# Reordering the seven products of a Strassen group, and when its weight sums are made

## The reference

```
h   = x + concat(mlstm(...), hgrn2(...)) @ w_out        # gates, conv, norms around it
h   = h + sigmoid(rms(h) @ w_pg) * (p @ w_pe);  x = rms(h)
proj = rms(x) @ w_in_2                                   # u, v, q, k, v_att, g_a, g_b
merged = sigmoid(g_a) * (y_a @ w_up_a) + sigmoid(g_b) * (y_b @ w_up_b)
x   = x + merged @ w_o
x   = x + (silu(h @ w_gate) * (h @ w_up)) @ w_ffn_out    # FFN_HIDDEN = 5632
x   = x + sigmoid(rms(x) @ w_ple_gate) * (p @ w_ple)
```

## Time and profile before

| | |
|---|---|
| three runs | 1892.29, 1894.62, 1895.87 us (median 1894.62) |
| the profiled execution | 1893.05 us, span of its instructions 1891.3 us |
| busy | TensorE 99%, VectorE 78%, ScalarE 60%, GpSimd 7% |
| granted TensorE clock | 0.999 of full on average |
| DMA | 535.95 MB, mean 283 GB/s |

### The profile page before, as it was taken

One profiled execution on the slowest core, in us unless ns is written; L12 is line 12 of the kernel. 1 busy time (PEld: TensorE's weight loads), 2 busy tenths in 40 slices (PEclk: granted clock), 3 DMA queues, 4 the chain that ended last, 5 costly groups with the idle time before them and its releaser, 6 DMA issues.

```text
span 1891.3 us, 23371 instructions
## 1 busy us (share of the span) xinstructions
PE 1877.2 (99%) x9018; PEld 1641.9 (87%) x9018; DVE 1471.8 (78%) x1591; ACT 1140.8 (60%) x1417; POOL 130.4 (7%) x156
## 2 busy tenths in 40 slices
PE   9999999999999999999999999999999999999998
PEld 8888888888888888888888888888888888888887
DVE  6889776655666677778888657988998999898865
ACT  7556445555566556566766455666766676666553
POOL 4000011000001100000000000000000000000000
PEclk9999999999999999999999999999999999999999
DMA  9799898999989879998797886788878887987653
GB/s 392 267 284 310 274 309 272 330 347 327 309 290 312 271 269 299 321 315 278 295 313 247 330 256 239 254 311 284 276 254 320 280 271 257 327 260 249 219 188 130
DMA packets 86815, 535.95 MB, mean 283 GB/s; under 512 B 10416, under 2 KB 11184, under 8 KB 40752
## 3 DMA queue, kind: packets, MB, share of 16 engines
q1 hardware_dynamic: 72736, 458.69, 63.3%
q0 software_dynamic: 13824, 75.50, 20.6%
q10 hardware_dynamic: 144, 0.26, 0.0%
HBM read 529.69 MB, written 105.38 MB: 336 GB/s over the span
## 4 chain that ended last, share of the span: by engine, by line
PE 90%; DVE 5%; DMA 3%; issue 1%; ACT 1%; POOL 0%; SPq 0%; ACTq 0%; DVEq 0%; POOLq 0%
PE acc L1359 44%; PE acc L1364 22%; PE aux L1724 12%; PE aux L1728 6%; DVE wlo L2556 2%; PE aux L1338 2%; DMA ple<-in_w_ffn_in 1%; DVE wlo L1876 1%; PE aux L1431 1%; DVE ple L2551 1%; DMA ple<-in_w_in 1%; DMA raw<-summed 1%; PE aux L1805 0%; ACT whi L928 0%; ACT whi L1177 0%
## 5 line engine op out<-in xcount | busy, mean ns | idle before, releaser
L1876 DVE TENSOR_TENSOR wlo<-raw,whi 128x1024 fp32r<-128x1024 f32 x512 | 623.8, 1226 | 296.4 <-ACT whi L928 288.4
L928 ACT ACTIVATE whi<-raw 128x1024 fp32r<-128x1024 f32 x511 | 534.0, 1054 | 449.8 <-PE acc L1364 414.1
L1359 PE MATMUL acc<-whi,actA_hi 128*128 128x512 f32 x892 | 344.0, 386 | 0.7 <-ACT whi L928 0.7
L1359 PE MATMUL acc<-whi,actA_lo 128*128 128x512 f32 x892 | 339.1, 380 | 0.0
L1359 PE MATMUL acc<-whi,actB_hi 128*128 128x512 f32 x796 | 304.5, 383 | 0.2 <-DVE actB_lo L2673 0.2
L1359 PE MATMUL acc<-whi,actB_lo 128*128 128x512 f32 x796 | 301.7, 379 | 0.0
L1177 ACT ACTIVATE whi<-ple 128x1024 fp32r<-128x1024 f32 x192 | 201.0, 1055 | 139.4 <-PE acc L1364 55.6
L2556 DVE TENSOR_TENSOR wlo<-ple,whi 128x1024 fp32r<-128x1024 f32 x192 | 230.2, 1220 | 31.3 <-ACT whi L1177 28.5
L1364 PE MATMUL acc<-wlo,actA_hi 128*128 128x512 f32 x892 | 229.1, 379 | 0.0
L1364 PE MATMUL acc<-wlo,actB_hi 128*128 128x512 f32 x796 | 204.4, 379 | 0.0
L2556 DVE TENSOR_TENSOR wlo<-raw,whi 128x1024 fp32r<-128x1024 f32 x144 | 174.2, 1220 | 30.6 <-ACT whi L1177 28.9
(11 more groups left out here) (366 smaller groups left out, 2377.0 us busy)
## 6 DMA issues: line engine op xcount, KB each, us to landing
raw<-in_w_in SPq DMA_DIRECT2D x108, 1024.0 KB, 7.3
raw<-in_w_ffn_out SPq DMA_DIRECT2D x44, 1024.0 KB, 6.9
summed<-in_w_ffn_in POOLq DMA_DIRECT2D x36, 1024.0 KB, 11.6
raw<-in_w_ffn_in SPq DMA_DIRECT2D x72, 512.0 KB, 7.9
ple<-summed SPq DMA_DIRECT2D x24, 1024.0 KB, 4.9
raw<-summed SPq DMA_DIRECT2D x48, 512.0 KB, 5.4
ple<-in_w_ffn_in SPq DMA_DIRECT2D x18, 1024.0 KB, 6.9
ple<-in_w_ffn_in POOLq DMA_DIRECT2D x36, 512.0 KB, 9.9
```

What stands on the lines that cost most here:

```text
L928: act.activation(whi[:, g % RING], raw_piece(g), ACT.Copy).then_inc(hi_ready, 1)
L1359: pe.matmul(acc2(n)[:, t, :], act[x][:, k + c, t * P:(t + 1) * P], woven(whi, g, c), start=(p == 0 and c == 0 and x == 0), stop=False)
L1876: dve.tensor_tensor(wlo[:, g % RING], raw_piece(g), whi[:, g % RING].bitcast(F32), ALU.subtract)\
```

## The change

- `S_ORDER` becomes M1, M2, M5, then M6 and M3 in turns (q by q), M7, M4. All that hung on "the last of M3" as the end of the four (`s_gates`, the gate's activation, the return of `resid`) now hangs on M7's last quarter, which stands where M3's last one stood. The wait for the forms of the activations is at M5 now.
- The copy `s_fifth` is made one piece earlier.
- The four DRAM sums at the first merge pieces go from `SUM_AT`; numbers 40 to 43 take the places in the output product (g 419 to 437), numbers 44 to 47 are at g 443, 449, 455 and 461, the first FFN pieces. Before the FFN's norm factor GpSimd issues those with g below `g_ffn` only.
- Three small ones: the norm factor's product at `L0 + 31`; the second half of `ml_cols` after the next piece (`ml_rows_spread`); the product of the slab uB 2 two pieces later.

```
-S_ORDER = [(m, q) for m in ("M1", "M2", "M7", "M5") for q in range(4)] \
-    + [("M6", 0), ("M6", 1), ("M3", 0), ("M6", 2), ("M3", 1), ("M6", 3), ("M3", 2), ("M3", 3)] + [("M4", q) for q in range(4)]
+S_ORDER = [(m, q) for m in ("M1", "M2", "M5") for q in range(4)] \
+    + [(m, q) for q in range(4) for m in ("M6", "M3")] + [(m, q) for m in ("M7", "M4") for q in range(4)]
...
-        SUM_AT += [PLAN.g_plan + 1 + 4 * i for i in range(4)]
         SUM_AT += [PLAN.g_out + 11 + 6 * i for i in range(4 * S_GROUPS - len(SUM_AT))]
...
                 if name == "ffn":
-                    add_in_dram(len(SUM_AT))
+                    add_in_dram(len([g for g in SUM_AT if g < PLAN.g_ffn]))
...
-                if g == S_AT[c, "M5", 3] + 3:
+                if g == S_AT[c, "M5", 3] + 2:
                     s_done(act, c, "M5")
...
-                for i in range(2):
-                    u = AUX[("bc", i)]
-                    free(u)
-                    for h in range(2):
-                        ins = pe.matmul(bank(u)[:, h * S:(h + 1) * S], sel[:, 2 * i + h, :], hrow[:, 3, :], start=True, stop=True)
-                    ins.then_inc(aux_full, 1)
+            def ml_rows_spread(i):
+                u = AUX[("bc", i)]
+                free(u)
+                for h in range(2):
+                    ins = pe.matmul(bank(u)[:, h * S:(h + 1) * S], sel[:, 2 * i + h, :], hrow[:, 3, :], start=True, stop=True)
+                ins.then_inc(aux_full, 1)
...
                     if (s, p) == (10, 7):
                         ml_cols()
+                        ml_rows_spread(0)
+                    if (s, p) == (11, 0):
+                        ml_rows_spread(1)
...
-                        if w == L0 + 30:
+                        if w == L0 + 31:
                             powered(dve, f"hB{half}")
...
-                s_done(dve, c, "M3")
+                s_done(dve, c, "M7")
...
-                        if g == slab_end(role, j) + (2 if slab_end(role, j) in PLAN.block_end else 3):
+                        last = slab_end(role, j)
+                        if g == last + (2 if last in PLAN.block_end else 5 if (role, j) == ("uB", 2) else 3):
                             u_product(role, j)
```

More of the change, by code:

```diff
@@ L801, in _ @@
                     sp.wait_ge(lo_ready, free + 1)
-                    sp.wait_ge(piece_used, S_AT[M_GROUPS - 1, "M3", 3] + 1)
+                    sp.wait_ge(piece_used, S_AT[M_GROUPS - 1, "M7", 3] + 1)
                     sp.wait_ge(sem("resid_held"), 16)
@@ L1224, in _ @@
                     s_copies(g, c)
-                    if g == S_AT[c, "M3", 3] + 7:
+                    if g == S_AT[c, "M7", 3] + 7:
                         act.wait_ge(sem("s_gate_in"), c + 1)
@@ L1296, in _ @@
                 split_hi(g)
-                if g == S_AT[S_GROUPS - 1, "M3", 3] + 7:
+                if g == S_AT[S_GROUPS - 1, "M7", 3] + 7:
                     s_silu(S_GROUPS - 1)
@@ L1699, in s_piece @@
                     pe.wait_ge(sem("tr_taken"), fills_before(g, "a"))
-                if m == "M7" and q == 0:
+                if m == "M5" and q == 0:
                     pe.wait_ge(sem("merge_forms_lo" if c < M_GROUPS else "forms_lo"), 4)
@@ L2635, in _ @@
                         s_up(c)
-                    if g == S_AT[c, "M3", 3] + 3:
+                    if g == S_AT[c, "M7", 3] + 3:
                         s_gates(c)
```

## The result

The changed kernel takes 1940.16 us (median of 6, 1937.51 to 1942.12), the kernel before 1894.37 us in the same comparison (median of 6, 1892.29 to 1895.87): ratio 1.0242, 95% interval 1.0229 to 1.0255. The forecast was 1886 us with a range of 1882 to 1893. It was wrong in sign and by 54 us. The case that happened is rival D, to which the prediction gave 0.07, and it came out more than twice as large as D's own price (54 us above the forecast, where D had 20).

What follows compares the result with a forecast made beforehand. TensorE was taken as the bound, busy 1877.2 of 1891.3 us, with only its losses to win: -6.9 + 0.7 - 0.6 - 1.6 = -8.4 from 1893.05 gives 1884.65, plus 1.57 to the runs' median, 1886 us; range 1882 to 1893.

Steps and rivals of the forecast that it cites:

- rival D: M7's last quarter late beside accumulating DMAs in every group, from a landing of 7.6 us on: 20 us lost, 1906; chance 0.07.
- Scaling 4.4 by 9.3 / 6.8 gives 6.0 us, which is hidden.: "Seventh" landing alone, scaled by b21's landing beside accumulating DMAs over b22's: under the 7.6 us available to M7's last quarter.
- the prediction's term for M7: M7's quarters, at distances of about 14.3, 13.0, 9.1 and 7.8 us, lose nothing; group 0's old 1.62 us go.
- The Trainium skill's rule: DMA engines alternate between queues with work: "seventh" up to 8.8 us, 1.2 us lost per group, 14 us, 1900 us in all.
- rival B: VectorE late in the stretch of sums, 0.4 to 0.9 us in each FFN group: 1890 to 1894 us; chance 0.12.
- M4, -5.3 us: M4's accumulating DMAs get 16.9 us of distance instead of 10.4, so all six M4 losses go.
- M7 of group 0, -1.6 us: Longer distances and no DRAM sums competing at the first merge pieces: group 0's loss of 1.62 us at M7 goes.
- The DRAM sums, "Cost 0; at worst 1.1 us": Four sums moved to the FFN's beginning cost nothing; at worst group 3 again loses what it lost, 1.1 us.
- rival C: DMAs stay late elsewhere, at M5 or M6's sums; half of 6.9 us returns, some at FFN's start: 1890 to 1893; chance 0.09.
- "Fifth" and b22, cost 0: Loads due sooner: "fifth" for M5 has 14.3 us, slowest landing 12.8; cost 0. b22's median landing 6.8 against 10 us.
- VectorE, +0.7 us: Sums and splits from M5's third quarter to M3's third: small losses over all groups, bounds 0 and 12 x 1.2 us.
- The norm factor's product and the gates' rows, -0.6 and -1.6: Product made behind the operands near 161 us: TensorE's wait goes, -0.6; gates' rows split in halves: clock stays up, -1.6 us.

Runs made afterwards that it cites:

- experiment 5: The changed kernel with GpSimd's twelve times four accumulating DMAs made plain, same place and bytes, the addition left out: 1891.39 us, ratio 0.9988 to the kernel before.
- experiment 4: The changed kernel with each group's third and fourth accumulating DMA issued later, when M7's first and second quarter are split: 1908.16 us, ratio 1.0071.
- experiment 9: As experiment 8, but in the order M1, M2, M7, M5 and M6 woven, M3, M4: 1891.85 us, ratio 0.9987 to the kernel before.
- experiment 10: The order of experiment 9 and the three small edits, with the DRAM sums where they were before the change: 1889.68 us, ratio 0.9975.
- experiment 11: As experiment 10, with the merge's four DRAM sums placed where the DMA share is lowest: 1887.64 us, ratio 0.9968 to the kernel before.
- experiment 1: The changed kernel with the old group order back; moved DRAM sums and small edits stay: 1897.78 us, ratio 1.0013 to the kernel before.
- experiment 8: The kernel before with the three small edits, the last eight DRAM sums all in the output product, and their copies no longer ahead of `resid` and `p` loads: 1897.17 us.
- experiment 6: The changed kernel with each accumulating DMA cut from 512 KB to 256 KB, half the addition left out: 1893.14 us, ratio 1.0001 to the kernel before.
- experiment 2: The changed kernel with the four DRAM sums back at the first merge pieces, new order kept: 1934.56 us, ratio 1.0213 to the kernel before.
- experiment 3: The changed kernel without the twelve groups' accumulating DMAs, the second term of M4's weights left out: 1890.13 us, ratio 0.9977 to the kernel before.
- experiment 7: The kernel before with the three small edits alone, order and sums as before: 1891.25 us, ratio 0.9987; 1890.27 us in one more run.

## Why the prediction was wrong

*The step that failed* is the landing of "seventh" in rival D: "Scaling 4.4 by 9.3 / 6.8 gives 6.0 us, which is hidden." With it the prediction's term for M7 counted no loss but the old one of group 0. Measured are 11.3 us for the third quarter and 10.2 for the last (medians of twelve), 5.9 and 7.0 for the first two. Three things were wrong in it.

- The ratio came from the wrong pair. b22's 6.8 us was no undisturbed landing: these loads were issued right behind a 1 MB load, with the DMA share at 0.89. And the scaling was not needed. b21's loads move the same 512 KB in the place to which "seventh" was to go, beside the accumulating DMAs, as the kernel before shows in group 3:

```profile
1217.49 1.85 POOL L898 DMA_DIRECT2D ple<-in_w_ffn_in  x2 [66.36 <-DVE wlo L2556]
...
1219.94 9.06 SPq L788 DMA_DIRECT2D raw<-in_w_ffn_in  x4
```

The last two accumulating DMAs follow at 1221.4 and 1226.0. The landings of these b21 loads are the 9.3 us of the earlier trace rows, and as they stand they are over D's 7.6 us.
- A ratio of landings is no sum of work. By the engine times of experiment 5 the burst of group 5 holds 4 x 2.9 for the accumulations, 4 x 1.4 for "seventh" and 2.8 for the std load, 20 us of all 16 engines. It starts at 1356.0, and its last quarter lands at 1380.2. M7's third quarter needed its weights at 1375.7 less ScalarE's 1.06, 18.6 us after the start. With plain DMAs in the same places (experiment 5) the burst is 14 us, and TensorE does not wait. The comparison is rough: what was issued up to and with the third quarter's load is only 15.7 us. But by its landing at 1378.6 the engines had worked 21 us (the shares of the stretches above), so the transfers issued behind it took their part, and in the first 8 us the share was only 0.57 and 0.92. Nothing in a sum over one transfer shows that; the sum over the burst does, and the prices were there in the earlier trace rows, if only roughly.
- The quarter looked at was the last, since its distance is the shortest. The third has 1.3 us more of it, but the end of its wait comes first, and then the last finds its weights nearly there.

The Trainium skill's rule, which the prediction weighed and set aside ("DMA: Bandwidth & Descriptors", Queues, rings and completion order), was nearer to the truth than my scaling, and still not enough: by it 4.4 us becomes up to 8.8, while the third quarter's landings are 11.3 us in the median and 12.6 at most. Experiments 4 and 5 show what it leaves out here: how many transfers the burst holds, and that those of the other queue take twice their bytes' time.

*The size.* D's 20 us took 1.7 us for each group. The waits at M7 are 31.3 us, some 2.8 us for each of eleven groups; with that come 7.8 us of clock, which D did not count, and VectorE's share: its splits, held up with ScalarE's, arrive in a heap, and the waits of TensorE's weight loads for `wlo` at L1731 are 12.1 us in 20 places against 4.7 in 8. Without the accumulating DMAs they are 2.4 in 4, so that is a consequence and not rival B.

*M4, -5.3 us:* right in mechanism, but the size was that of one execution. In the changed kernel 0.4 us of wait for its loads is left, and the order of experiments 9 to 11, which gives M4 two more quarters and keeps M7 where it was, has it as a gain: 1889.68 against 1891.25 us with sums and small edits the same (two comparisons, whose intervals overlap), and by rows no wait for `ple<-in_w_ffn_in` where the small edits alone left 29.4 us. By starts M4 loses 3.7 us in the trace of the small edits alone and nothing in that of experiment 10.

*M7 of group 0, -1.6 us:* half right. It had been the sums (experiments 1, 8 and 11: no loss with the sums moved away, the first two in the old order). But the same M7 waits 2.94 us, in its third quarter, by the new order.

*The DRAM sums, "Cost 0; at worst 1.1 us":* wrong, 5.5 us. It went by the number of pieces between the sums and did not ask what else is issued there. At the FFN's beginning the first group loads its `r1` and four slots at once. It is the place that rival C names, with 1890 to 1893 us, 4 to 7 above the forecast.

*"Fifth" and b22, cost 0:* right apart from group 3, where M5 loses 1.85 and 0.87 us by starts, beside the sums. The 12.8 us of the earlier trace rows are passed there; the landings of all 24 "fifth" loads of the changed kernel are

```profile
DMA to landing us min/median/max: 4.6/4.9/17.3
```


*VectorE, +0.7 us:* can't be read off, since its waits in the changed kernel follow from the late loads. With plain DMAs, in the same order, the waits for `wlo` are 5.0 us in 9 places, 0.3 more than before. Right as far as that shows.

*The norm factor's product and the gates' rows, -0.6 and -1.6:* right, -2.5 us together with the third small edit, as far as an interval of -4.2 to -0.8 can say. What the prediction took there from the Trainium skill ("TensorE: Matmul & The Clock Gate", Part 1), that the place varies from run to run, the page says of the clock's rise. That its fall varies too is shown by the traces (below); the sum did not use it.

## What to carry to other kernels

Where a change brings loads nearer to each other, add up the DMA time of the whole burst, each transfer at its own price, and compare it with the time from the burst's first issue to its first need (here 20 against 18.6 us with waits, 14 without); neither a landing time nor the mean DMA share tells it. An accumulating DMA goes into that sum at twice its bytes. Where loads of the same size already stand beside the same traffic, take their landing as it is, without scaling, as the least. When TensorE waits some microseconds, the half clock behind the wait may come on top (8.7 us behind five waits here).

## What the runs showed of the hardware

- A DMA that adds to its destination took 2.9 us of all 16 DMA engines for 512 KB, a plain one from the same queue 1.4 us, and one that adds 256 KB 1.5 us (experiments 5 and 6). The median landings are 9.1 and 5.7 us (all 48).
- With the DMA share at 1.0, the rate in the burst was 271 to 307 GB/s with accumulating DMAs. With plain ones it was, in the same burst

```profile
1346.00:1350.00 4.00, 4.00 (x20) 3.52 (x19) 3.82 (x4) 2.87 (x4) 0.53 (x1) 1.00 1.01 414
1350.00:1354.00 4.00, 4.00 (x20) 3.49 (x20) 1.67 (x2) 2.05 (x3) 0.00 (x0) 1.00 1.01 394
```

- In the changed kernel the clock fell to 0.50 behind waits of TensorE of 3.88, 4.29, 4.09 and 3.76 us (groups 2, 3, 5 and 8), and did not behind those of 2.94 (group 0), 2.15 and 2.11 us (groups 4 and 7). Behind group 9's wait of 2.46 us it fell all the same. It fell behind 5.22 us in experiment 1; in experiment 2 behind 3.12 us and not behind 3.21.
- Whether it falls differs between executions at the same place. Up to a start near 220 us TensorE waits 2.61 or 2.62 us in each of thirteen traces. Behind it the clock fell in eight (experiments 1, 3, 4, 5, 6, 8, 9 and 11) and not in five (before, changed, experiments 2 and 10 and the profile of experiment 7); at 0.66 over 5 us it costs 1.7 us. The stretch in the kernel before, and in experiment 1 (busy us by engine, then granted clock, DMA share, GB/s):

```profile
220.00:225.00 5.00, 5.00 (x32) 4.60 (x33) 4.75 (x10) 0.42 (x1) 0.00 (x0) 1.00 0.80 164
```

```profile
220.00:225.00 5.00, 5.00 (x25) 4.72 (x24) 4.75 (x10) 0.00 (x0) 0.00 (x0) 0.66 0.77 157
```

- What stays open besides is why an accumulation costs twice. The Trainium skill says in "DMA: Bandwidth & Descriptors" (Rules for kernel authors) that an accumulating DMA reads its destination and writes it later; two reads in place of one would fit the factor of two if the reads set the pace, but no run separates that from another reason.
